# Chunked attention: the copy of the turned values is moved ahead in ScalarE's order

## The reference

```python
def chunked_relpos_attention(q, k, v, rel_bias):
    # q, k, v: (B, L, 16, 64); chunks of 64 positions
    s = jnp.einsum('bcqhd,bckhd->bhcqk', qc, kb).astype(jnp.float32) * scale
    s = s + bias[None, :, None]
    s = jnp.where(valid[None, None, :, None, :], s, -jnp.inf)
    p = jax.nn.softmax(s, axis=-1).astype(v.dtype)
    o = jnp.einsum('bhcqk,bckhd->bcqhd', p, vb)
    return o.reshape(b, l, h * dh)
...
    o_a = chunked_relpos_attention(q.reshape(shp), k.reshape(shp), v.reshape(shp), rel_bias)
    o_a = o_a * jax.nn.silu(z_a)
```

## Time and profile before

| | |
|---|---|
| median of 3 runs | 3478.31 us (3476.17 to 3479.16) |
| the profiled execution | 3474.39 us |
| its span, first to last instruction | 3472.5 us |
| TensorE matmuls busy | 3218.1 us, 93% |
| vector engine, ScalarE, GpSimd busy | 38%, 36%, 39% |
| mean granted TensorE clock | 0.967 |
| chunked attention, first score product to last gated product | 1905.7 to 2153.2 us |

### The profile page before, as it was taken

One profiled execution on the slowest core, in us unless ns is written; L12 is line 12 of the kernel. 1 busy time (PEld: TensorE's weight loads), 2 busy tenths in 40 slices (PEclk: granted clock), 3 DMA queues, 4 the chain that ended last, 5 costly groups with the idle time before them and its releaser, 6 DMA issues.

```text
span 3472.5 us, 47346 instructions
## 1 busy us (share of the span) xinstructions
PE 3218.1 (93%) x18030; PEld 2437.6 (70%) x18030; DVE 1319.2 (38%) x1699; ACT 1237.5 (36%) x1675; POOL 1362.7 (39%) x645
## 2 busy tenths in 40 slices
PE   6999998989998988899998997998999999999898
PEld 5777776767776866465555775786777877877686
DVE  4556655233233133888883332313211111111212
ACT  3333333244444232444442443323333233333322
POOL 2222221332232454877772221345433333333242
PEclk9999998999999988899999998999999999999999
DMA  4211110222122423122223222242222222222243
GB/s 162 75 51 52 56 56 29 83 78 67 60 66 79 147 91 104 46 65 72 69 72 102 73 83 75 87 155 97 92 81 83 79 84 79 85 79 80 68 131 102
DMA packets 92996, 286.03 MB, mean 82 GB/s; under 512 B 9776, under 2 KB 14160, under 8 KB 92368
## 3 DMA queue, kind: packets, MB, share of 16 engines
q1 hardware_dynamic: 64512, 233.14, 21.5%
q10 hardware_dynamic: 28368, 51.20, 4.4%
HBM read 261.21 MB, written 23.09 MB: 82 GB/s over the span
## 4 chain that ended last, share of the span: by engine, by line
PE 67%; issue 19%; POOL 6%; DVE 4%; ACT 3%; PEld 1%; DMA 1%; ACTq 0%; PEldq 0%; POOLq 0%; DVEq 0%; SPq 0%
PE ps L288 16%; PE ps L290 15%; PE ps L289 15%; POOL w_lo L2314 4%; PE ps L1887 2%; PE ps L661 2%; PE ps L662 2%; PE ps L663 2%; POOL act_lo L460 1%; PE ps L1411 1%; PE ps L1879 1%; PE ps L1428 1%; PE ps L707 1%; PE ps L305 1%; PE ps L1586 1%
## 5 line engine op out<-in xcount | busy, mean ns | idle before, releaser
L2314 POOL TENSOR_TENSOR w_lo<-raw,w_hi 128x1024 fp32r<-128x1024 f32 x442 | 1078.5, 2442 | 2015.6 <-ACT w_hi L472 2014.0
L288 PE MATMUL ps<-act_hi,w_hi 128*128 128x512 f32 x2624 | 1039.5, 396 | 35.8 <-POOL w_lo L2314 21.5
L290 PE MATMUL ps<-act_lo,w_hi 128*128 128x512 f32 x2624 | 1026.7, 391 | 0.0
L289 PE MATMUL ps<-act_hi,w_lo 128*128 128x512 f32 x2624 | 1026.2, 391 | 0.0
L472 ACT ACTIVATE w_hi<-raw 128x1024 fp32r<-128x1024 f32 x442 | 465.9, 1055 | 811.3 <-PE ps L290 394.3
L288 PEld LDWEIGHTS ps<-act_hi,w_hi 128*128 128x128 f32 x2624 | 496.0, 189 | 178.4 <-issue 72.5
L290 PEld LDWEIGHTS ps<-act_lo,w_hi 128*128 128x128 f32 x2624 | 495.4, 189 | 105.3
L289 PEld LDWEIGHTS ps<-act_hi,w_lo 128*128 128x128 f32 x2624 | 496.3, 189 | 101.0 <-issue 0.7
L358 DVE TENSOR_TENSOR mix<-ps,arena 128x512 f32 (+1 forms) x48 | 33.2, 692 | 442.0 <-PE ps L290 399.4
L661 PE MATMUL ps<-act_hi,w_hi 128*128 128x512 f32 x384 | 158.0, 411 | 0.0
L933 PE MATMUL ps<-act_hi,w_hi 128*128 128x512 f32 x352 | 155.3, 441 | 0.0
(11 more groups left out here) (358 smaller groups left out, 4067.9 us busy)
## 6 DMA issues: line engine op xcount, KB each, us to landing
raw<-stream SPq DMA_DIRECT2D x442, 512.0 KB, 3.5
arena<-residual ACTq DMA_DIRECT2D x48, 256.0 KB, 2.7
residual<-mix ACTq DMA_DIRECT2D x32, 256.0 KB, 2.1
mix<-x ACTq DMA_DIRECT2D x4, 1024.0 KB, 9.7
residual<-arena ACTq DMA_DIRECT2D x4, 1024.0 KB, 5.9
kept_qk<-mix ACTq DMA_DIRECT2D x16, 256.0 KB, 2.3
arena<-kept_qk ACTq DMA_DIRECT2D x16, 256.0 KB, 3.4
out<-arena ACTq DMA_DIRECT2D x4, 1024.0 KB, 5.0
```

What stands on the lines that cost most here:

```text
L288: pe.matmul(dst, w_hi[:, slot, j, :], act_hi[:, kt, :], start=first, stop=False)
L289: pe.matmul(dst, w_lo[:, slot, j, :], act_hi[:, kt, :], start=False, stop=False)
L290: mm = pe.matmul(dst, w_hi[:, slot, j, :], act_lo[:, kt, :], start=False, stop=last)
L2314: nc.gpsimd.tensor_tensor(w_lo[:, s, :, :], src[:, s % 2, :, :], w_hi[:, s, :, :].bitcast(F32), ALU.subtract).then_inc(split_done, 1)
```

## The change

On ScalarE the copy of the turned values leaves the start of a pair and becomes a function of its own, `values(u)`. It is called for pair u+1 near the end of pair u: behind a wait for the value products, ahead of the wait for "mix" and of `take(u + 1, 1)`. For the first pair it is called between `take(0, 0)` and `take(0, 1)`. The copy no longer counts as a step of `ev_act` but has a semaphore `ev_copied`, for which TensorE waits ahead of the score products.

```diff
-        ev_act = Steps(sem("ev_act"), "vn " + " ".join(f"e{h}_{b}" for h in range(2) for b in EV_ORDER)
+        ev_act = Steps(sem("ev_act"), " ".join(f"e{h}_{b}" for h in range(2) for b in EV_ORDER)
                        + " pt0 pt1")
+        ev_copied = sem("ev_copied")
...
                 pe.wait_ge(qk_loaded[j], (u - j) * 16 + 32)
-                A.wait(pe, "vn", u)
+                pe.wait_ge(ev_copied, u + 1)
                 V.wait_before(pe, u)
...
             def unit(u, j, more):
                 A.start(u)
-                act.wait_ge(ev_turned, u + 1)
-                if not (isinstance(u, int) and u == 0):
-                    S.wait(act, "pv", u - 1)
-                A.mark(nc.scalar.activation(ev_v, ps[:, 7, :], ACT.Copy), "vn")
                 if more:
                     load_qk(u + 1, 1 - j)
...
                 if more:
+                    S.wait(act, "pv", u)
+                    values(u + 1)
                     V.wait(act, "mix", u)
                     take(u + 1, 1)
                 A.finish()
+
+            def values(u):
+
+                act.wait_ge(ev_turned, u + 1)
+                nc.scalar.activation(ev_v, ps[:, 7, :], ACT.Copy).then_inc(ev_copied, 1)
...
             load_qk(0, 0)
             take(0, 0)
+            values(0)
             take(0, 1)
```

## The result

The changed kernel takes 3456.3 us (median of 4 runs, 3452.7 to 3456.9) against 3478.7 for the kernel before beside it: a ratio of 0.993, 95% interval 0.9913 to 0.9947. That is 22.4 us less. The profiled execution took 3456.74 us with a span of 3454.9.

The account below looks back on a forecast made before the run. TensorE, busy 93% of the span, was taken as the bound, its score products waiting for ScalarE's late copy. Seams 16.5 + clock 4.9 = 21.4 us, from the median 3478.31 to 3456.9 us; range 3452 to 3463.

Parts of the forecast that it names:

- The seam: Seven seams between pairs: with the copy early, scores start 2.36 us sooner at each, 16.5 us in all.
- The idle-column value: TensorE's idle at the seven seams as the profile's column gives it: 15.3 us, low end of the seam term.
- The clock: Three of seven stretches between pairs ran partly at 1.2 GHz; without the idle this ends, 4.9 us (bounds 0 and 4.9).
- Rival 1: Chunked attention: the gap at the seams goes but the slower clock stays, 3461.8 us; chance 15%.
- What was costed at nothing: Chunked attention: moved casts and split, q and k load, softmax chain under the split, first and last pair: 0 us.
- rival 2: Seams: the vector engine's bias adds are held under GpSimd's split, 7 x 1.57 = 11.0 us back, 3467.9 us; chance 6%.
- The three gaps named "issue": Three score-product waits, 6.5 us together, put down to "issue"; the forecast counted them as the copy's, like the other four seams.
- rival 3: Seams: the three "issue" gaps are TensorE's own fetching of new code, so only four seams gain, 3465.6 us; chance 5%.
- Rivals 4 and 5: 4: scores' q and k loads end as late, 3478, 5%; 5: first pair's gate tile too late, slower, 2%.
- The level: Whole kernel: 21.4 us off the median of three runs, 3478.31 us, gives 3456.9 us.

Follow-up runs that it names:

- the half move: Against the changed kernel, the copy stands behind the gate and ahead of the second weight cast, a pause of 1.2 us; 3468.2 us, ratio 0.9968.
- The series above: Changed kernel (no pause) against versions pausing TensorE at the seams: 1.2 us, 3468.2 us; 1.7 us, 3471.5 us; 4.1 us, 3501.2 us; the kernel before pauses 2.2 us.

## Why the prediction was right

**The seam.** The forecast was that the copy alone held the scores, and that nothing else was as late. The waits of L1587 show it, and the half move shows how much each part of the delay was worth. The step was put at 2.36 us and measured 2.27: the scores start 0.32 us behind the last gemm matmul (1996.80 to 1997.12), not 0.23 as the transposes do. It is the one term that was mis-sized: 7 x 0.09 = 0.6 us of 16.5, pairs of 29.53 us for 29.42. The idle-column value of 2.20 a seam, given as the low end, lies 0.07 below what was measured.

**The clock.** 4.9 us were booked on the guess that three equal pauses of 2.2 us had brought the clock down and the others not. The trace of the kernel before already says where the slow pieces begin, in the score products right behind the pause, which take 2.43 us at full clock:

```profile
2001.03 4.09 PE L1586 MATMUL ps<-arena 64*128 64x384 f32 x16 [2.20 <-ACT arena L1650]
...
2034.48 3.44 PE L1586 MATMUL ps<-arena 64*128 64x384 f32 x16 [2.20 <-ACT arena L1650]
...
2099.64 3.73 PE L1586 MATMUL ps<-arena 64*128 64x384 f32 x16 [2.17 <-issue]
```

The series above bears it out. The casts, the splits and the copy are the same in the changed kernel and in those with pauses of 1.7 and 4.1 us. Only the pause differs, and the number of falls goes from none to one to seven. Nor does "none" rest on one trace: in nine traces of kernels without the pause (the changed one three times, and the six with other edits) the clock is 1.00 in all 54 stretches behind a seam. Rival 1, in which the pause had nothing to do with it, falls. At pauses of 1.7 and 2.2 us a piece at 1.2 GHz comes now and then and costs 1.6 to 1.7 us each time; at 1.2 us none came in the one trace taken.

The Trainium skill (TensorE: Matmul & The Clock Gate, "Why this matters for your kernels") warns only of longer pauses than these. The seven falls behind 4.1 us agree with it, the three behind 2.2 us do not: shorter pauses than it names can bring the clock down, and here the measurement decides.

Seams (7 x 2.27 = 15.9) and clock (4.9) together make 20.8 us by these terms, 20.6 by the stretches.

**What was costed at nothing** stayed so. The bias adds take 0.96 to 0.97 us under the split (rival 2 would have had up to 1.57 more). The three gaps named "issue" closed with the other four, so rival 3 falls: they were the copy's too, and the column had only failed to name it. The scaling still ends just ahead of the transposes (2006.91 + 3.44 = 2010.35 for 2010.51), with the same slack of about 0.15 us:

```profile
2006.91 3.44 DVE L1714 TENSOR_SCALAR arena<-arena,ev_st 128x128 f32<-128x128 f32 x4
...
2010.28 0.39 PE L290 MATMUL ps<-act_lo,w_hi 128*128 128x512 f32 x1
2010.51 2.35 PE L1599 MATMUL ps<-ident,arena 128*128 128x128 f32 x20
```

In the first pair the first exp comes 4.97 us behind the scores, 4.98 by the forecast (1910.7 less 1905.72). Rivals 4 and 5 fall as well: no score product waits for q and k, and no gemm of the first pair waits for its weights.

The Trainium skill (ScalarE: Activation LUTs, "What ACT_TABLE_LOAD costs") adds a drain to each load for another set. It doesn't show here: in the first pair two loads of 1.28 us are followed by their activations within 0.02 us.

**The level.** The forecast from the median, 3456.9, was within 0.6 us. Part of that is luck: three medians of this same kernel are 3456.3, 3454.9 and 3457.4 (beside 3478.7, 3477.8 and 3481.6 for the kernel before), and the stages ahead of the attention end anywhere from 1901.5 to 1911.5 us in the traces of this study.

## What to carry to other kernels

An engine's list is a queue: put what another engine will wait for ahead of what has to wait for that engine itself. Here 0.6 us of copying, whose input was ready 7 us before, stood behind a gate that waited for TensorE's last gemm. To find such places, read who releases the bottleneck after each short idle, and ask when that instruction's own inputs were ready. A short pause of TensorE costs more than its length when the clock falls after it, so look at the granted clock of the stretch behind each pause.

## What the runs showed of the hardware that was not expected

- A pause of TensorE of about 2 us can bring its clock down, and of equal pauses not every one does: behind seven pauses each it fell three times at 2.2 us, once at 1.7 us and seven times at 4.1 us, and it began with the first matmuls behind the pause. Once it fell behind two shorter pauses, 0.78 and 1.34 us, with 0.66 us of transposes between.
- The length of stages whose code is the same varies between executions by several us (first scores at 1901.5 to 1911.5 us; 8.7 of these 10 us are TensorE's own busy time for the same matmuls, 1730.0 against 1738.6), so an edit of a few us is read from the stretch that it touches rather than from a median of four runs.
- Score products with 64 rows start 0.32 us behind a full matmul of 512 columns, transposes 0.23 us.
